# A streaming encoder trunk: output projections of six units by seven products on token halves

## The reference, cut to what matters

```
proj = h @ w_in[i]                                  # short conv, attention, retention, RWKV-7 inputs
mix = concatenate([y_conv, y_swa, y_ret, y_rwkv]) @ w_out[i]      # 1024 x 1024: the output projection
h = layer_norm(ALPHA * h + mix, ln1_g[i], ln1_b[i])
h = layer_norm(ALPHA * h + conv_glu_ffn(h, w_up, conv_w, w_down), ln2_g[i], ln2_b[i])
```

## Time and profile before

| | us |
|---|---|
| median of 3 runs | 3058.86 |
| lowest and highest | 3054.92, 3059.01 |
| the profiled execution, own time | 3060.03 |
| its span, first to last instruction | 3057.9 |

### The profile page before, as it was taken

How to read it: one execution, slowest core, us unless ns; L and a number is a source line. 1 busy time by engine, 2 the same in 40 slices (tenths; PEclk the granted TensorE clock), 3 DMA queues, 4 the chain that set the end, 5 groups by cost and what they waited for, 6 DMA issues and landing times.

```text
span 3057.9 us, 64432 instructions
## 1 busy us (share of the span) xinstructions
PE 3016.3 (99%) x27228; PEld 2764.3 (90%) x27228; DVE 1525.5 (50%) x3657; ACT 946.0 (31%) x2387; POOL 207.5 (7%) x301
## 2 busy tenths in 40 slices
PE   8999999999999999999999999999999999999998
PEld 7788778889898899989989899999999989999998
DVE  4345552346633465346553356545566255663662
ACT  3324440134412244024341244303343043421320
POOL 0111010011101110010010101000000000000000
PEclk9999999999999999999999999999999999999999
DMA  7577477788978989888797888986768857677887
GB/s 258 168 205 212 120 208 221 223 233 289 312 240 258 287 270 319 237 259 284 224 312 212 261 280 258 297 288 191 261 204 267 287 183 243 210 260 258 299 295 251
DMA packets 226828, 760.19 MB, mean 249 GB/s; under 512 B 24800, under 2 KB 44384, under 8 KB 226288
## 3 DMA queue, kind: packets, MB, share of 16 engines
q1 hardware_dynamic: 189328, 620.80, 60.9%
q0 software_dynamic: 37216, 135.28, 18.0%
HBM read 744.33 MB, written 136.31 MB: 288 GB/s over the span
## 4 chain that ended last, share of the span: by engine, by line
PE 91%; DMA 3%; DVE 3%; ACT 2%; issue 0%; SPq 0%; ACTq 0%; DVEq 0%
PE psum L1874 29%; PE psum L1307 27%; PE psum L1897 10%; PE psum L1933 8%; PE psum L1444 6%; DMA slots<-wsum 2%; PE psum L1301 2%; DMA slots<-in_weights 1%; PE psum L1323 1%; PE psum L1622 1%; PE psum L1647 1%; PE psum L1634 1%; PE psum L1573 1%; PE psum L1695 1%; PE psum L1808 1%
## 5 line engine op out<-in xcount | busy, mean ns | idle before, releaser
L1307 PE MATMUL psum<-hT,slots 128*128 128x256 f32 (+1 forms) x2880 | 658.9, 387 | 3.1 <-ACT hT L861 2.1
L1307 PEld LDWEIGHTS psum<-hT,slots 128*128 128x128 f32 x2880 | 541.6, 190 | 97.2 <-issue 5.5
L1874 PE MATMUL psum<-tsum,slots 128*128 128x128 f32 (+1 forms) x4928 | 607.9, 277 | 13.8 <-ACT raw L1220 4.9
L1874 PEld LDWEIGHTS psum<-tsum,slots 128*128 128x128 f32 x4928 | 573.1, 191 | 30.9 <-issue 20.3
L1874 PE MATMUL psum<-hT,slots 128*128 128x128 f32 (+1 forms) x3696 | 453.5, 276 | 3.7 <-DMA slots<-wsum 2.8
L1874 PEld LDWEIGHTS psum<-hT,slots 128*128 128x128 f32 x3696 | 432.7, 192 | 6.5 <-DMA slots<-wsum 3.5
L1897 PE MATMUL psum<-gT,slots 128*128 128x256 f32 (+1 forms) x1408 | 309.9, 383 | 0.0
L1897 PEld LDWEIGHTS psum<-gT,slots 128*128 128x128 f32 x1408 | 267.0, 190 | 40.9
L1307 PE MATMUL psum<-mixT,slots 128*128 128x256 f32 (+2 forms) x1024 | 226.4, 381 | 1.2 <-DVE hT L2046 1.2
L1307 PEld LDWEIGHTS psum<-mixT,slots 128*128 128x128 f32 x1024 | 194.2, 190 | 29.7 <-issue 1.5
L2046 DVE SCALAR_TENSOR_TENSOR hT<-hT,psum 128x256 f32<-128x256 f32 (+2 forms) x96 | 40.6, 424 | 348.1 <-PE psum L1897 249.7
(11 more groups left out here) (327 smaller groups left out, 3531.0 us busy)
## 6 DMA issues: line engine op xcount, KB each, us to landing
slots<-in_weights SPq DMA_DIRECT2D x667, 512.0 KB, 4.5
slots<-wsum SPq DMA_DIRECT2D x308, 512.0 KB, 4.5
wsum<-in_weights POOLq DMA_DIRECT2D x132, 512.0 KB, 6.7
slots<-wsumi SPq DMA_DIRECT2D x64, 512.0 KB, 4.4
slots<-wsumd SPq DMA_DIRECT2D x64, 512.0 KB, 4.4
wsum<-wsum POOLq DMA_DIRECT2D x44, 512.0 KB, 7.9
wsumi<-in_weights POOLq DMA_DIRECT2D x24, 512.0 KB, 7.8
wsumd<-in_weights POOLq DMA_DIRECT2D x24, 512.0 KB, 9.2
```

What stands on the lines that cost most here:

```text
L1307: ins = mm(psum[:, i % 2, :n], lhsT, rhs, start=k == 0, stop=k == len(pairs) - 1)
L1874: ins = mm(dst[:, e * n:(e + 1) * n], w[:, (4 * e + k) * P:(4 * e + k + 1) * P], moving[s][k], start=s in (0, 1, 5) and e == 0 and k == 0, ...
```

## The change

The output projections of u = 1 to 6 (`OUT_FAST`) take fourteen steps `os0_0` to `os1_6` in place of eight dense blocks. PE's `out_by_seven` uses banks, slots and order as the up stage does, and puts the mean's sum after the second step and the variance's after the thirteenth. VectorE makes the token sums of mixT into `tsum` (`mix_sums(u + 1)`, four operations) in the down stage of u, after its slot 20 of 24 or its step 12 of 14; it adds each of the fourteen products to hT (`residual_quarter`) and takes one step of the later norm after all but the first two, and the rest behind the last. The out blocks that stay dense (u = 0 and 7) are stored in the layout of quarters, so they come in pairs of slots.

The weight sums are two more lists of sixteen DMAs, `out_sums(0)` and `out_sums(1)`. The points of the first lie in the first unit's up stage, those of the second in the down stage of u = 2 (nine) and in the input stage of u = 4 (seven). POOL issues the first list after `rwkv(1)` and before the further up sums, the second in its turn for u = 3, after the up sums with points below the first up block of u = 3 and before `rwkv(4)`. SP waits for all sixteen before the first summed block of u = 1 and of u = 4. The four semaphores of the down sums become one, with the same order.

The up sums keep their number. Since `sum_points` spreads them over blocks, and the out stages have more blocks, their points move: 6 to 9 in the out stage of u = 1, 8 to 11 in those of u = 2, 3 and 4, and fewer elsewhere. In the input stage of u = 4 the last of them is at block `sk` (before: `sk` and `sv`).

```
+OUT_FAST = [1, 2, 3, 4, 5, 6]
+def out_spare(l):
+    if l == 0:
+        return [AT[0, f"up{f}"] for f in range(14, 36)]
+    return [i for i, (u, name) in enumerate(BLOCKS) if (u == 2 and name[:2] in ("dn", "ds")) or (u == NCH and name in MIX_PART)]
...
+            def out_sums(l):
+                steps, at = out_spare(l), 0
+                def in_time():
+                    nonlocal at
+                    at += 1
+                    return steps[len(steps) * (at - 1) // 16]
+                for group in range(2):
+                    for kind, first in (("S1", "A21"), ("S3", "A11"), ("S2", "A11"), ("S4", "A12")):
+                        yield in_time()
+                        g.dma_start(out_block(l, kind, group), out_block(l, first, group), max_dma_last_dim=4096).then_inc(S["wo_made"], 16)
+                for kind, more, count in (("S1", "A22", 128), ("S3", "A21", 128), ("S2", "S1", 192), ("S4", "S2", 224)):
+                    for group in range(2):
+                        yield in_time()
+                        g.wait_ge(S["wo_made"], 256 * l + count)
+                        g.dma_start(out_block(l, kind, group), out_block(l, more, group), accum_op=ALU.add,
+                                    max_dma_last_dim=4096).then_inc(S["wo_made"], 16)
...
                 if 1 < u <= NCH:
                     sums_until(1, first_up)
+                if u == NCH - 1:
+                    sums_until(5, first_up)
                 if u + 1 < NU:
                     rwkv(u + 1)
+                if u == 0:
+                    sums_until(4, AT[1, out_names(1)[0]])
...
+            def out_by_seven(u, x):
+                n = span_of(u, 0)[1] // 2
+                old, new = [y[:, 0:n] for y in x], [y[:, n:2 * n] for y in x]
+                t1, t3, t2, t4 = ([tsum[:, j, k, :n] for k in range(4)] for j in range(4))
+                moving = [old[:4], t1, t2, new[4:], t3, old[4:], t4]
+                for g in range(2):
+                    base = AT[u, f"os{g}_0"]
+                    for s in range(7):
+                        w = next_slot()
+                        bank_free(base + s)
+                        if (g, s) == (0, 1):
+                            pe.wait_ge(S["osum"], 4 * (OUT_FAST.index(u) + 1))
+                        dst = product_at(u, base, s)
+                        for e in range(2):
+                            for k in range(4):
+                                ins = mm(dst[:, e * n:(e + 1) * n], w[:, (4 * e + k) * P:(4 * e + k + 1) * P], moving[s][k],
+                                         start=s in (0, 1, 5) and e == 0 and k == 0, stop=k == 3, skip_group_check=True)
+                        ins.then_inc(S["blk"], 1)
+                        if (g, s) == (0, 1):
+                            ln_mean(2 * u - 1)
+                        if (g, s) == (1, 5):
+                            ln_var(2 * u - 1)
...
+            def mix_sums(u):
...
+                v.wait_ge(S["blk"], AT[u - 1, up_names(u - 1)[-1]] + 1)
+                tt(t1, b11, b12, ALU.subtract).then_inc(S["osum"], 1)
+                tt(t3, b22, b12, ALU.subtract).then_inc(S["osum"], 1)
+                v.wait_ge(S["osum"], before + 2)
+                stt(t2, t3, -1.0, b11, ALU.mult, ALU.subtract).then_inc(S["osum"], 1)
+                v.wait_ge(S["osum"], before + 3)
+                stt(t4, t2, -1.0, b21, ALU.mult, ALU.subtract).then_inc(S["osum"], 1)
...
+                if u in OUT_FAST:
+                    for g in range(2):
+                        for s in range(7):
+                            out_step(u, g, s)
+                            if g or s > 1:
+                                advance(program, 1)
+                    rest(program)
+                    return
```

More of the change, by code:

```diff
@@ L71, in down_names, with out_names @@
     return [f"ds{g}_{s}" for g in range(2) for s in range(7)] if u in DN_FAST else [f"dn{m}" for m in range(KD)]
+def out_names(u):
+    return [f"os{g}_{s}" for g in range(2) for s in range(7)] if u in OUT_FAST else [f"out{m}" for m in range(KD)]
 def down_yields(u):
@@ L89, in width @@
 def width(u, name):
-    if name[:3] == "out" or name[:2] == "up":
+    if name[:2] in ("ou", "up"):
         return span_of(u, 0)[1]
@@ L176, in all_blocks @@
     for u in range(NU - 1):
-        out += [(u, f"out{m}") for m in range(KD)]
+        out += [(u, name) for name in out_names(u)]
         out += [(u + 1, name) for name in in_order(u + 1)]
@@ L180, in all_blocks @@
         if u == NU - 2:
-            out += [(u + 1, f"out{m}") for m in range(KD)]
+            out += [(u + 1, name) for name in out_names(u + 1)]
         out += [(u, name) for name in down_names(u)]
@@ L261, in all_uses @@
         elif name[:3] == "out":
-            out.append((l, N_IN + int(name[3:]), u, name, None))
+            m = int(name[3:])
+            if m % 2 == 0:
+                out += [(l, N_IN + m + half, u, f"out{m + 1}", None) for half in range(2)]
+        elif name[:2] == "os":
+            g, s = map(int, name[2:].split("_"))
+            kind = STEPS7[s]
+            which = (l, g, SUMS.index(kind)) if kind[0] == "S" else N_IN + 4 * g + QUADS.index(kind)
+            out.append((l, which, u, name, None))
         elif name[:2] == "up":
@@ L642, in _ @@
                     source = weights[l, which] if STEPS7[int(name[-1])][0] == "A" else wsum[l, which[0], which[1]]
+                elif name[:2] == "os":
+                    if name == "os0_1" and u in (1, NCH):
+                        sp.wait_ge(S["wo_made"], 256 * (l + 1))
+                    source = weights[l, which] if STEPS7[int(name[-1])][0] == "A" else wsumo[which]
                 elif name[:2] == "is":
@@ L766, in down_sums @@
                             g.dma_start(down_block(kind, group, b), down_block(first, group, b),
-                                        max_dma_last_dim=4096).then_inc(S["wd_copy"], 16)
-                for kind, more, ready, count, done in (("S1", "A22", "wd_copy", 384, "wd_first"), ("S3", "A21", "wd_copy", 384, "wd_first"),
-                                                       ("S2", "S1", "wd_first", 192, "wd_second"), ("S4", "S2", "wd_second", 96, "wd_third")):
+                                        max_dma_last_dim=4096).then_inc(S["wd_made"], 16)
+                for kind, more, count in (("S1", "A22", 384), ("S3", "A21", 384), ("S2", "S1", 576), ("S4", "S2", 672)):
                     for group in range(2):
@@ L810, in input_sums, with out_block @@
                         g.dma_start(in_block("S2", w - 2), in_block("S1", w - 2), accum_op=ALU.add, max_dma_last_dim=4096).then_inc(S["wi_second"], 16)
-            sums += [down_sums(), input_sums()]
-            pending += [next(sums[2]), next(sums[3])]
+            def out_block(l, kind, group):
+                if kind[0] == "A":
+                    return weights[l, N_IN + 4 * group + QUADS.index(kind)]
+                return wsumo[l, group, SUMS.index(kind)]
+            def out_sums(l):
[14 more added lines that the diff above has]
+                                    max_dma_last_dim=4096).then_inc(S["wo_made"], 16)
+            sums += [down_sums(), input_sums(), out_sums(0), out_sums(1)]
+            pending += [next(sums[k]) for k in range(2, 6)]
             def sums_until(l, limit):
```

70 lines of the change are left out of this document (48 added, 22 removed).

## The result

The changed kernel took 3119.43 us (median of 4; 3116.77 to 3123.43), the kernel before 3058.94 beside it on the same chip (3054.92 to 3060.52): ratio 1.0197, interval 1.0183 to 1.0210, so 60.5 us slower. The forecast was 3077 us with a range up to 3097. The direction and both places were right; the size was not. The profiled execution took 3123.43 us, its span is 63.8 us longer than the span of before.

The account below looks back on a forecast made before the run. TensorE, busy 99% of the span, was taken to bound the kernel. Terms -15.7 + 1 + 9.5 + 22 + 1 = +17.8 us on the profiled 3060.03 gave 3077.8, forecast as 3077 us, range 3056 to 3097.

Parts of the forecast that it names:

- 2.62 us less per unit, 15.7 in all: Out stages: fourteen seven-product steps replace eight dense blocks, saving PE 2.62 us per unit, 15.7 us for six units.
- VectorE hidden: Out and down stages: VectorE's added residuals, norm steps and token sums (2.8 us per unit) would not hold PE.
- The handover, 1 us in all: Out stage's end into the next stage: later norm finishes late; bounds 0 and 1 us a unit, 1 us taken altogether.
- The DMA engines in the out stages, 9.5 us, bounds 0 and 23: Second to fifth unit's out stages: more loads and denser sums make PE wait, 9.5 us altogether, between 0 and 23.
- my worst case of 5.8: Out stages beside sums: loads every 2.91 us at worst, losing at most 5.8 us per unit.
- My own count of engine work: Out stage: fourteen loads at 1.36 us and eleven sums at 2.06 make 41.7 us of engine work in 25 us.
- The rival of even sharing: Out stages: sums and loads share evenly throughout, costing 5.8 us in each of four units, some 3090 us; chance 0.20.
- its sign: Out stages: loads landing 10 us or more after issue from the third step on would decide for even sharing.
- POOL in front of the fifth unit's RWKV part, 22 us: Sixteen second-layer sums stand before POOL's RWKV operations after sk; PE waits 22 us, bounds 8 and 30.
- a restart of 1: After PE's rest of 22 us in the fifth unit's RWKV part, slower matmuls cost 0 to 1.9 us, taken as 1.
- The chance of 0.78 for slower: Whole kernel: probability 0.78 that the change is slower by more than 0.2%, against 0.13 within it and 0.09 faster.

Follow-up runs that it names:

- experiment 2: Changed kernel with the up sums taken out of the out stages and spread over the other blocks: 3097.76 us, ratio 1.0124.
- experiment 6: Changed kernel, second list behind POOL's RWKV operations, no up sums in out stages, later norm finished inside the out stage: 3059.59 us, ratio 0.9993.
- experiment 7: Against experiment 1, only four of each seven out steps are points, so out stages have 6, 8, 8, 8 up sums as before: 3073.99 us.
- experiment 5: Against experiment 1, the up sums' accumulating DMAs issued as plain copies, additions left out: 3075.51 us, ratio 1.0053.
- experiment 1: Changed kernel with POOL issuing the second list of output sums behind its RWKV operations of the fifth unit: 3087.69 us, ratio 1.0094.
- Experiments 2 and 3: The first has its own line; the second is the changed kernel with the edits of experiment 1 and experiment 2 together: 3061.6 us, ratio 1.001.
- experiment 8: Against experiment 6, seven products only in the fifth to seventh unit, second list alone, up sums back in dense out stages: 3058.95 us, ratio 1.0.

## Why the prediction was wrong, point by point

- *2.62 us less per unit, 15.7 in all*: right. 2.61 us in the sixth and seventh unit, and the same pace in the first layer once the sums are away (experiment 2).
- *VectorE hidden*: right. No wait of L1918 for VectorE is in the profile, and the stages of 25.88 us leave no room for one.
- *The handover, 1 us in all*: too small; it is near the upper bound, 1 us a unit. The input stages of u = 6 and 7 show 1.1 and 0.5; experiment 6 shows that it was this.
- *The DMA engines in the out stages, 9.5 us, bounds 0 and 23*: **the step that failed.** The four stages lost 35.5 us (25.0 longer, and 10.5 not won), above the upper bound. The step priced a load beside sums at 2.91 us, from 5.40 MB in 30 us. That was an average over a window in which the software queue was at times empty, and the equal shares there (50.8% and 47.5%) I read as turns of equal time. Where accumulating sums are queued all the time, turns are of equal bytes: 1.00 and 1.02 MB, at 66.1% and 38.2%. So the steps that wait for a load come once per 3.8 us. The trace of before showed it inside the window of the earlier trace rows, in the stretch from 1575 to 1587 us, where sums are queued all the time:
```profile
q0 software_dynamic: 467, 1.55, 67.1%
q1 hardware_dynamic: 464, 1.68, 37.6%
```
Equal packets at 67% and 38%; in the 8 us behind it q0 has 11% and q1 76.8%, which is what brought the mean of the loads up to 5.40 MB. The rule of the Trainium skill that I had weighed (DMA: Bandwidth & Descriptors, Queues, rings and completion order: a turn is a packet) agrees with this and not with my reading of it. I wrote that the trace agrees and gave 50.8% and 47.5%, but a turn of one packet shows in equal packets, and the earlier trace rows has 864 and 1478. And the discount from the worst case, for gaps between POOL's waits, was my choice, and too large: of the four stages only u = 2, at 5.9 us, lost no more than about my worst case of 5.8.

My own count of engine work, which stood in the same paragraph (1.36 us per load, 1.34 per copy, 2.06 per mean sum), would have come nearer, had I not set it aside for slots and lag:

| | engine work, worked out, u = 1; u = 2 to 4 | measured, u = 1, 2, 3, 4 |
|---|---|---|
| changed kernel (9; 11 sums) | 37.6; 41.7 | 34.7, 31.8, 35.7, 37.0 |
| experiment 7 (6; 8 sums) | 31.4; 35.5 | 28.0, 29.8, 33.4, 34.4 |
| experiment 5 (9; 11 copies) | 31.1; 33.8 | 29.5, 28.7, 29.8, 30.8 |
| experiment 2 (none) | 19.0 | 25.9, 25.9, 26.5, 28.1 |

The stages are the engine work less 1 to 7 us (10 in one), and not under PE's 25.9; full slots at the start and lagging sums absorb the difference. With a fixed 6.8 us for five full slots, the changed kernel's four stages come to 135.5 us for 139.2 measured, but those of experiments 7 and 5 to 112.0 and 106.9 for 125.6 and 118.8. So the count says that a stage is over, and not closely by how much. The rival of even sharing was nearer than the forecast, but its price failed too: loads did land 12 to 13 us after issue, its sign, but it had 5.8 us a unit, and the measured loss is 8.7, 5.9, 9.9 and 10.9 us.

- *POOL in front of the fifth unit's RWKV part, 22 us, and a restart of 1*: the mechanism right, in its place and order; the size 29.1 us against before, 32.2 against experiment 1 (in which the wait of 2.84 us at the end of the earlier trace rows is gone too), 33.4 by its parts. The chain ended at +57.3 where I had +54.2. The need I had taken from the wrong row: L1634 at 1470.74, while `first_product`, which waits for POOL, is L1622 at 1465.66, five microseconds earlier, +27.3 and not +32.3. In the changed kernel it came at +32.7 after all, since the loads of the products ahead of it were late beside the copies (0.72 and 2.45 us of wait in the rows above). So the wait itself, 24.7, looks like my 22, and 5.7 us more lie in front of it under another name. The restart cost 3.0 us, and not 1.
- *What no step had*: the other stages, +14.5 us in the input and up stages. Of these, 8.7 us are longer waits of PE for weights (the up stage of u = 3 aside), and 1.6 the handover of the last two units. Experiments 2 and 3 show that sums moved out of one stage are partly paid in another. How much is due to the moved points and how much to the lists themselves stays open.
- *Together*: the forecast was +17.8 us, and the profiled execution has +63.8. Of the 46 us between them, 26 are the DMA step, 6 the wait for POOL with its restart, and 13.5 the stages that no step had.

The chance of 0.78 for slower was well placed; the range was too narrow because the upper end of one term rested on an average.

## What to carry to other kernels

Before a stage is shortened, add up its DMA work in engine time, the background DMAs included, each kind at its own price, and compare this with the new length of PE's work: here 41.7 us of it stood against 25. An average over a window in which one queue is at times empty is no upper bound for what the other gets. Work appended to an in-order list is paid by the next urgent entry behind it: look for that entry, find the very instruction that waits for it, and put the new work behind it. And the form that needs fewer products is worth having only where its extra weights have room: in this kernel, the last two units.

## What the runs showed of the hardware

- An accumulating DMA from DRAM to DRAM takes turns with a load packet for packet, in equal bytes, but holds the engines for 1.8 times as long per byte in the same stretch (66.1% for 1.00 MB, 38.2% for 1.02 MB; before, 67.1% for 1.55 MB and 37.6% for 1.68 MB). A plain copy of the same size delays the loads beside it by about a third as much (steps 2.5 us apart in place of 3.8, against 1.8 undisturbed).
- TensorE's granted clock fell to its lower level over the long wait and shortly after it, and in a shorter form in an out stage with a wait of 2.2 us. The windows after (start and end, length, busy times of five engines, granted clock, DMA share, GB/s):
```profile
985.00:993.00 8.00, 5.83 (x36) 5.43 (x35) 2.09 (x6) 0.47 (x1) 1.88 (x3) 0.80 1.02 355
...
1490.00:1520.00 30.00, 7.60 (x73) 7.23 (x72) 5.98 (x16) 2.22 (x6) 5.00 (x7) 0.70 0.83 214
1520.00:1530.00 10.00, 7.66 (x54) 7.31 (x55) 1.94 (x7) 0.69 (x2) 2.12 (x5) 0.54 0.68 125
1502.00:1529.00 27.00, 6.66 (x45) 6.31 (x46) 1.69 (x6) 0.69 (x2) 4.70 (x8) 0.50 0.68 144
```
The last has a granted clock of 0.50, the level of 1.2 of 2.4 GHz. PE had stopped at 1497.6 us and was at work again from 1522.3, so some 7 us of its work ran at that level: 16 records there took 3.78 us for 1.95 of the same shape. So this wait cost its length and 3.0 us behind it. The waits of 2.2 us here and 3.0 us in experiment 8 were followed by 3.46 and 3.78 us for 16 such records.
